# The front of a two-block transformer kernel in a new order, with other rings for its weights

## What is computed

```
def first_block(x, ...):
    n1 = rms_norm(h, norm1_gain)
    proj = n1 @ w_in                    # q_lat 512, kv_lat 256, k_pe 64, q_swa 1024, k_swa 128, v_swa 128
    q_lat, kv_lat, k_pe, q_swa, k_swa, v_swa = split(proj)
    o_mla = mla_group(...)              # 8 heads of 128+64, q and k from the latents, norm per head, rope
    o_swa = swa_group(...)              # 16 query heads of 64, 2 kv heads, window 128, bias by distance, sinks
    mixed = concat([rms_norm(o_mla, g), rms_norm(o_swa, g)])
    h = h + mixed @ w_out
    h = h + peer(rms_norm(h, norm2_gain), ...)   # product keys, top 16 of 128 x 128, 16384 experts
    return h
```

## Time and profile before

| | us |
|---|---|
| median of 3 runs | 3338.53 (3335.76 to 3339.82) |
| the profiled execution | 3337.88 |
| its span, first to last instruction | 3335.7 |
| PE busy | 3250.5 (97%) |
| VectorE busy | 2020.4 (61%) |
| ScalarE busy | 1490.8 (45%) |
| POOL busy | 539.9 (16%) |

### The profile page before, as it was taken

One profiled execution on the slowest core, in us unless ns is written; L12 is line 12 of the kernel. 1 busy time (PEld: TensorE's weight loads), 2 busy tenths in 40 slices (PEclk: granted clock), 3 DMA queues, 4 the chain that ended last, 5 costly groups with the idle time before them and its releaser, 6 DMA issues.

```text
span 3335.7 us, 38691 instructions
## 1 busy us (share of the span) xinstructions
PE 3250.5 (97%) x15278; PEld 2704.2 (81%) x15278; DVE 2020.4 (61%) x2922; ACT 1490.8 (45%) x1876; POOL 539.9 (16%) x321
## 2 busy tenths in 40 slices
PE   8888999999999999999999999999999999999998
PEld 7677898788888888888888888888888788888886
DVE  6755568884444456666666665565465655555556
ACT  5434444444444444444444444445444544444443
POOL 0100004787778700000000000000000000000000
PEclk9889999999999999999999999999999999999999
DMA  6553456888888877777776665555666566666664
GB/s 207 179 206 95 145 174 189 200 206 207 209 213 205 208 275 247 244 246 245 241 243 217 183 198 183 158 176 172 189 189 199 176 188 189 189 189 189 189 189 151
DMA packets 215092, 658.71 MB, mean 197 GB/s; under 512 B 56128, under 2 KB 56272, under 8 KB 212352
## 3 DMA queue, kind: packets, MB, share of 16 engines
q1 hardware_dynamic: 165680, 598.71, 57.6%
q0 software_dynamic: 49232, 57.54, 7.7%
HBM read 620.38 MB, written 35.78 MB: 197 GB/s over the span
## 4 chain that ended last, share of the span: by engine, by line
PE 88%; DVE 8%; ACT 3%; issue 1%; DMA 0%; DVEq 0%; ACTq 0%; SPq 0%
PE bank L1554 86%; PE bank L1616 2%; DVE wlo L1981 2%; ACT whi L1760 1%; ACT M L1802 1%; DVE AL L2027 0%; DVE M L2267 0%; DVE M L2273 0%; DVE R L2459 0%; ACT M L1750 0%; DVE M L2271 0%; DVE M L2269 0%; DVE M L2084 0%; DVE TMP L2050 0%; DVE M L2284 0%
## 5 line engine op out<-in xcount | busy, mean ns | idle before, releaser
L1981 DVE TENSOR_TENSOR wlo<-raw,whi 128x1024 fp32r<-128x1024 f32 x1101 | 1343.8, 1223 | 1082.1 <-ACT whi L1760 1077.7
L1760 ACT ACTIVATE whi<-raw 128x1024 fp32r<-128x1024 f32 x1101 | 1159.8, 1058 | 1301.5 <-PE bank L1554 1265.0
L1554 PE MATMUL bank<-whi,BH 128*128 128x512 f32 x2344 | 932.5, 398 | 12.8 <-DVE wlo L1981 7.7
L1554 PE MATMUL bank<-whi,BL 128*128 128x512 f32 x2344 | 915.3, 390 | 0.0
L1554 PE MATMUL bank<-wlo,BH 128*128 128x512 f32 x2344 | 913.8, 390 | 0.0
L1554 PE MATMUL bank<-whi,AH 128*128 128x512 f32 (+1 forms) x1952 | 772.4, 396 | 22.5 <-DVE AL L2027 15.2
L1554 PE MATMUL bank<-whi,AL 128*128 128x512 f32 (+1 forms) x1952 | 762.6, 391 | 0.0
L1554 PE MATMUL bank<-wlo,AH 128*128 128x512 f32 (+1 forms) x1952 | 762.0, 390 | 0.0
L2524 POOL DMA_INDIRECT scr_g<-M x256 | 495.0, 1934 | 437.3 <-issue 396.5
L1554 PEld LDWEIGHTS bank<-whi,BH 128*128 128x128 f32 x2344 | 440.9, 188 | 106.2 <-DVE wlo L1981 12.4
L1554 PEld LDWEIGHTS bank<-whi,BL 128*128 128x128 f32 x2344 | 440.5, 188 | 94.3
(11 more groups left out here) (240 smaller groups left out, 1600.6 us busy)
## 6 DMA issues: line engine op xcount, KB each, us to landing
raw<-in_peer_u SPq DMA_DIRECT2D x256, 512.0 KB
raw<-in_peer_v SPq DMA_DIRECT2D x256, 512.0 KB
raw<-in_w_in SPq DMA_DIRECT2D x160, 512.0 KB
raw<-in_w_up SPq DMA_DIRECT2D x128, 512.0 KB
raw<-in_w_down SPq DMA_DIRECT2D x128, 512.0 KB
raw<-in_w_out SPq DMA_DIRECT2D x64, 512.0 KB
raw<-in_w_in_a SPq DMA_DIRECT2D x32, 512.0 KB
scr_g<-M POOLq DMA_DIRECT2D x8, 2048.0 KB, 29.8
```

The source lines that it names most:

```text
L1554: return e.matmul(outp, l, r, start=start, stop=stop)
L1760: e.activation(whi[:, n % NH, :], raw[:, n % NR, :], ACT.Copy).then_inc(s_hi, 1)
L1981: e.tensor_tensor(wlo[:, n % NH, :], raw[:, n % NR, :], bf(whi[:, n % NH, :]), ALU.subtract).then_inc(s_lo, 1)
```

## The change

The eight pieces of `swa_queries(1)` move from behind w_q_b to behind w_kv_b 0, 1, and w_kv_b 2, 3 (the values) to behind w_q_b 4, 5. `bias_gen` may run from the last w_q_b gemm on. `head_norm`'s work on VectorE is three calls with yields between them, and `q_side` has one yield less behind it. `q_scale` is a task. The MLA stage no longer waits for `rows` and `halves`; its extra buffers come by a task. OM is turned in the MLA stage, as its units' outputs are done, and OS beside the first half of w_out. hold=4 is dropped in w_out. The rings have 3 raw buffers, 4 high and 4 low parts instead of 5, 3 and 3.

```diff
-    NR, NH, NST = 5, 3, 1080
+    NR, NH, NST = 3, 4, 1080
...
-        plan("w_kv_b", 0, 4)
+        plan("w_kv_b", 0, 2)
+        plan("w_in_a", 24, 8)
         plan("w_q_b", 4, 2)
+        plan("w_kv_b", 2, 2)
         plan("w_q_b", 0, 4)
-        plan("w_in_a", 24, 8)
...
-                go("head_scale", tmp, x, U, L, mul, stat(2 * U), stat(2 * U), fresh("DVE", ta))
-                tv = up("DVE", "head_scaled")
+                ss, r = stat(2 * U), stat(2 * U)
+                go("head_sum", tmp, U, ss, fresh("DVE", ta))
+                tv = up("DVE", "head_summed")
                 halves.give(TMP[:, 0:512], tv)
                 halves.give(TMP[:, 512:1024], tv)
-                box.append(tv)
+                yield
+                go("head_root", ss, U, L, mul, r, fresh("DVE", tv))
+                tv = up("DVE", "head_root")
+                yield
+                go("head_scale", x, U, L, r, fresh("DVE", tv))
+                box.append(up("DVE", "head_scaled"))
...
-                go("load_piece", n_load[0])
-                n_load[0] += 1
+                if j < NR:
+                    go("load_piece", n_load[0])
+                    n_load[0] += 1
...
+                def above(n):
+                    pair, qb, kb, c = chunks[n]
+                    go("above", n % 2, qb, kb, c, fresh("DVE", t_pos, tk[n - 2] if n >= 2 else x_read))
+                    t2[n] = up("DVE", "above")
+
+                above(0)
+                yield
+                above(1)
+                yield
...
+                    go("bias_mm", bank, n % 2, BD[:, 0:64], fresh("PE", t2[n], t_steps, bfree))
+                    tk[n] = up("PE", "bias_looked_up")
+                    yield
+                    go("bias_mask", bank, pair, c, fresh("DVE", tk[n], pair_free[pair]))
                     bias_done.append(up("DVE", "bias_masked"))
                     misc.give(bank, bias_done[-1])
+                    if n + 2 < 12:
+                        above(n + 2)
...
             def q_scale():
+                while len(t_ssq) < 6:
+                    yield
+                yield
...
-            for j in range(4):
+
+            def keys(j):
                 pair, b, last = gemm("w_kv_b", j, 2, BH[:, 4:6, :], BL[:, 4:6, :], nKV)
-                if j < 2:
-                    ts, free = take(krows)
-                    te = evac2(pair, b, last, lambda t: ts[:, t, :], free, t_kv, r=r_kv)
-                    tasks.append(k_nope(ts, te, j))
-                else:
-                    t_v += evac2(pair, b, last, lambda t: VM[:, t, 512 * (j - 2):512 * (j - 2) + 512], x_read, t_kv, r=r_kv)
+                ts, free = take(krows)
+                te = evac2(pair, b, last, lambda t: ts[:, t, :], free, t_kv, r=r_kv)
+                tasks.append(k_nope(ts, te, j))
                 step()
-            kv_free = [last]
-            tasks.append(k_rope())
-
-            for j in (2, 0, 1):
+
+            def values(j):
+                pair, b, last = gemm("w_kv_b", 2 + j, 2, BH[:, 4:6, :], BL[:, 4:6, :], nKV)
+                t_v.extend(evac2(pair, b, last, lambda t: VM[:, t, 512 * j:512 * j + 512], x_read, t_kv, r=r_kv))
+                step()
+                return last
+
+            def queries(j):
                 pair, b, last = gemm("w_q_b", 2 * j, 4, BH, BL, nQ)
                 ts, free = take(qrows)
                 te = evac2(pair, b, last, lambda t: ts[:, t, :], free, t_lat, r=r_lat)
                 tasks.append(q_nope(ts, te, j) if j < 2 else q_rope(ts, te, j))
                 step()
 
+            kv_free = []
+            keys(0)
+            keys(1)
+            a_free.append(swa_queries(1))
+            tasks.append(k_rope())
+            queries(2)
+            values(0)
+            kv_free.append(values(1))
+            queries(0)
...
+            idle.append(bias_gen())
+            queries(1)
+            tasks.append(q_scale())
             tasks.append(pairs_freed())
-            idle.append(bias_gen())
-            a_free.append(swa_queries(1))
             lend_banks()
             go("gate_blank")
             t_blank = up("POOL", "gate_blank")
             for c in range(8):
                 go("gate_clear", c, fresh("POOL", t_blank))
                 t_clear = landing("gate_cleared")
-            while len(t_ssq) < 6:
+            while len(qt_done) < 6 or len(kt_done) < 8 or not t_rq:
                 step()
-            q_scale()
-            while len(qt_done) < 6 or len(kt_done) < 8 or len(rows.free) < 2 or len(halves.free) < 2:
...
+            def more_rows():
+                while len(rows.free) < 2:
+                    yield
+                r_over = [f for _, f in rows.free]
+                for i in range(4):
+                    pml.give(Rf[:, 2048 + 512 * i:2560 + 512 * i], r_over)
+
+            tasks.append(more_rows())
+            om_done, mla_scored = {}, []
...
+            def turned_heads(x, marks, n_marks, g0, k, done):
+
+                while len(mla_scored) < 6:
+                    yield
+                for k0 in range(0, 8, 2):
+                    while len(marks(k0)) < n_marks:
+                        yield
+                    yield from trans_split(lambda kt, t: x[:, t, 128 * (k0 + kt):128 * (k0 + kt) + 128], 2, hl(AH, k + k0),
+                                           hl(AL, k + k0), lambda kt: GC[:, g0 + k0 + kt:g0 + k0 + kt + 1], marks(k0),
+                                           mla_scored, done)
+
+            nM, nS = [], []
             tasks.append(pipelined([mla_unit(0, 0), mla_unit(0, 4)] + [mla_unit(1, h) for h in range(0, 8, 2)], 6, 6))
+            tasks.append(turned_heads(OM, lambda k0: [om_done[u] for u in ((0, 4 * (k0 // 4)), (1, k0)) if u in om_done],
+                                      2, 22, 0, nM))
             finish_idle()
-            assert len(bias_done) == 12
+            assert len(bias_done) == 12 and len(nM) == 4
...
-            tasks.append(turned_heads(OM, lambda k0: [om_done[0, 4 * (k0 // 4)], om_done[1, k0]], 22, 0, nM))
+            tasks.append(turned_heads(OS, lambda k0: [os_done[u] for u in ((0, 4 * (k0 // 2)), (1, 2 * k0), (1, 2 * k0 + 2))
+                                                      if u in os_done], 3, 30, 8, nS))
...
-                pair, b, last = gemm("w_out", 4 * j, 8, AH, AL, nM, hold=4, mid=True)
+                pair, b, last = gemm("w_out", 4 * j, 8, AH, AL, nM, mid=True)
...
-            tasks.append(turned_heads(OS, lambda k0: [os_done[0, 4 * (k0 // 2)], os_done[1, 2 * k0], os_done[1, 2 * k0 + 2]],
-                                      30, 8, nS))
...
-                pair, b, last = gemm("w_out", 16 + 4 * j, 8, AH[:, 8:16, :], AL[:, 8:16, :], nS, hold=4)
+                pair, b, last = gemm("w_out", 16 + 4 * j, 8, AH[:, 8:16, :], AL[:, 8:16, :], nS)
...
-            def head_scale(tmp, x, U, L, mul, ss, r, ready):
-                for mark in ready:
-                    e.wait_ge(*mark)
-                then(e.tensor_reduce(ss.rearrange("p (t u) -> p t u", t=2), tmp, AX.X, ALU.add))
-                e.wait_ge(s_vec, at[0])
-                then(root(ss, 2 * U, L, r, mul))
-                e.wait_ge(s_vec, at[0])
+            def head_sum(tmp, U, ss, ready):
+                for mark in ready:
+                    e.wait_ge(*mark)
+                e.tensor_reduce(ss.rearrange("p (t u) -> p t u", t=2), tmp, AX.X, ALU.add).then_inc(sem("head_summed"), 1)
+
+            def head_root(ss, U, L, mul, r, ready):
+                for mark in ready:
+                    e.wait_ge(*mark)
+                root(ss, 2 * U, L, r, mul).then_inc(sem("head_root"), 1)
+
+            def head_scale(x, U, L, r, ready):
+                for mark in ready:
+                    e.wait_ge(*mark)
                 r4 = r.rearrange("p (t u) -> p t u", t=2).unsqueeze(3).to_broadcast([128, 2, U, L])
```

More of the change, by code:

```diff
@@ L593, in bias_gen @@
                 t2, tk = {}, {}
[L594 to L602, removed]
+                def above(n):
[6 more added lines that the diff above has]
+                yield
+                for n, (pair, qb, kb, c) in enumerate(chunks):
                     while pair_free[pair] is None:
@@ L605, in bias_gen @@
                     bank, bfree = yield from wait_for(misc)
-                    go("bias_mm", bank, (n - 1) % 2, BD[:, 0:64], fresh("PE", t2[n - 1], t_steps, bfree))
-                    tk[n - 1] = up("PE", "bias_looked_up")
+                    go("bias_mm", bank, n % 2, BD[:, 0:64], fresh("PE", t2[n], t_steps, bfree))
+                    tk[n] = up("PE", "bias_looked_up")
                     yield
-                    go("bias_mask", bank, pair, c, fresh("DVE", tk[n - 1], pair_free[pair]))
+                    go("bias_mask", bank, pair, c, fresh("DVE", tk[n], pair_free[pair]))
                     bias_done.append(up("DVE", "bias_masked"))
                     misc.give(bank, bias_done[-1])
+                    if n + 2 < 12:
+                        above(n + 2)
             idle.append(x_squares())
```

(29 more changed lines are left out.)

## The result

The changed kernel takes 3342.43 us (median of 20 runs, 3340.06 to 3350.39) against 3336.7 us of the kernel before in the same sessions: a ratio of 1.0019 [1.0012, 1.0026]. It is slower, by 5.7 us. I had forecast 3299; 43 us are missing.

The account below looks back on a forecast made before the run. TensorE, busy 3250.5 of 3335.7 us, was the bound, so only its idle or lower-clock time could be gained. Terms -17 - 6 - 15 + 5 - 6 = -39 against 3337.88 gave 3299 us, range 3281 to 3318.

Parts of the forecast that it names:

- Part 1: Second half of w_out: OS turned beside the first half, so the gemms no longer wait for turned rows; -17 us (15 to 18).
- Part 5: Rings, 5+3 to 3+4: low-part waits between 400 and 800 us go, -6 (-3 to -7); main loop holds, 0 (to +4).
- The load that I dated: Worst load in a gate fetch, issued at 1252.44, released ScalarE 10.7 us later; taken to leave PE 0.9 us.
- rival (d): Gate fetches: three raw buffers too few, 3 us lost at each of 16 fetches, 48 in all; 3347 us, chance 0.04.
- Part 4: Front: clears of scr_g move from 145 to about 42.5 us and share DMA with weight loads; +5 us (0 to +15).
- rival (b): Front: the clears starve the weight loads, PE loses about 15 us instead of 5; 3309 us, chance 0.16.
- Part 3: Stage A, last long projection to first MLA scores: VectorE's idle time goes, 99.9 becomes 85 us; -15 (-23 to -8).
- part 2: MLA and first half of w_out: early turning removes AL waits and most half-clock spells; -6 us (-2 to -9).
- The two waits I aimed at: PE's stage A waits: 5.09 us behind head_scale at 108.86, 6.96 for the last swa query's chain; reordering should remove both.
- rival (c): Stage A: a new wait replaces the removed one, so it gives 3 us instead of 15; 3311 us, chance 0.12.
- Rival (a): Front: loads and clears share DMA evenly, so moving the clears costs nothing; 3294 us, chance 0.15.
- rival (e): w_out: turning of OS still ends behind the first half, taking back 10 us; 3309 us, chance 0.03.

## Why the prediction was wrong

**Part 1, second half of w_out (-17): right**, by mechanism and size (-17.7). No AL wait stands in it any more.

**Part 5, the parts of the ring (-6): right, and too small.** Of the twelve wlo waits of the routing one of 0.5 us is left: PE is busy 499.55 of 500 us against 494.20, and after gains 7.9 us between 400 and 800. The runs give 9.7, with the fetches spread.

**Part 5, the main loop (0): wrong, and it decides the sign.** The failed sentence is "From issue to use a piece had ... now 6 (13.9)". It takes the ring of parts as full whenever a fetch begins. Here is the first of the 14 later fetches of after, by engine (start, us, instruction, idle before):

```profile
1209.66 0.55 POOL L2577 DMA_DIRECT2D M<-scr_a  x1 [51.86 <-DVE AL L2411]
1210.19 0.91 POOL L2578 DMA_DIRECT2D M<-scr_g  x1
...
1210.88 0.33 SPq L2617 DMA_DIRECT2D raw<-in_peer_v  x1
1211.53 0.92 SPq L2623 DMA_DIRECT2D scr_a<-M  x1
...
1208.01 0.63 ACT L1788 ACTIVATE AH<-M 128x512 fp32r<-128x512 f32 x1 [1.48 <-DVE M L2404]
1208.55 1.99 ACT L1798 ACTIVATE whi<-raw 128x1024 fp32r<-128x1024 f32 x2
1210.98 1.06 ACT L1798 ACTIVATE whi<-raw 128x1024 fp32r<-128x1024 f32 x1 [0.45 <-DMA raw<-in_peer_v]
1219.21 1.06 ACT L1798 ACTIVATE whi<-raw 128x1024 fp32r<-128x1024 f32 x1 [7.16 <-DMA raw<-in_peer_v]
...
1210.91 0.50 PE L1592 MATMUL bank<-whi,BH 128*128 128x512 f32 x1 [0.55 <-DVE wlo L2019]
1221.67 0.63 PE L1592 MATMUL bank<-whi,AH 128*128 128x512 f32 x1 [2.31 <-DVE wlo L2019]
```

ScalarE's steps for the gate wait for VectorE (1.48 here; in both kernels these waits sum to some 136 us), the splits behind them come late, and then three splits run almost in a row. At 1210.9 PE has just waited for a part: nothing is spare. The three made then last 3 x 2.76 = 8.3 us, to 1219.2. The load issued at 1210.88 releases ScalarE at 1219.21, its low part is done 2.3 us later, and PE starts at 1221.67 after 2.31 us. So it had 8.5 us from issue to use, not 13.9, and an ordinary load beside a fetch was enough; I had wanted one of over 11.6. With five raw buffers, at the same place, two pieces more had landed when the burst began. PE's one wait there is the 0.44 at the handing over, and ScalarE's next split waits for PE, not for a load:

```profile
1208.26 0.50 PE L1592 MATMUL bank<-whi,BH 128*128 128x512 f32 x1 [0.44 <-DVE wlo L2019]
```

```profile
1211.39 1.06 ACT L1798 ACTIVATE whi<-raw 128x1024 fp32r<-128x1024 f32 x1 [2.41 <-PE bank L1592]
```

It is so at nearly every fetch: 12 of the 14 are followed, 10 to 13 us after their issue, by one wait of PE for a low part (0.3 to 2.7 us). Counted piece by piece (12 matmuls each) in the traces, the first load issued beside a fetch had 8.3 to 10.8 us until its use in after, 11.0 with four raw buffers and 13.8 with five. It needs its own time, 8.6 us beside a fetch in after (median; 11.7 the longest), and 2.3 for the split. So five buffers are just enough, four nearly, and three are not.

The trace of before had this to show. The load that I dated (issued at 1252.44) and the one ahead of it, beside the same fetch, were used at 1267.23 and 1264.51 (SP, then PE):

```profile
1250.71 0.33 SPq L2573 DMA_DIRECT2D raw<-in_peer_v  x1
...
1264.51 0.39 PE L1554 MATMUL bank<-whi,AH 128*128 128x512 f32 x1
...
1267.23 0.39 PE L1554 MATMUL bank<-whi,AH 128*128 128x512 f32 x1
```

These are 14.8 and 13.8 us where my count of pieces said 16.6 for both: the ring was short by up to a piece already. Less one piece for the new ring, 12.0 and 11.0 are left, against the 10.7 + 2.3 = 13.0 that the dated load needed. Its margin was -1 us and not 0.9.

The waits of ScalarE show the turn as a whole (us in total, times, longest). Before, from 1178 to 1830 us, they were for PE, and only 9.8 us for loads of peer_v:

```profile
ACT whi L1760 <- PE bank L1554: 215.1, 138, 2.4
```

After, in the same stretch:

```profile
ACT whi L1798 <- DMA raw<-in_peer_v: 213.3, 123, 8.5
...
ACT whi L1798 <- PE bank L1592: 18.5, 9, 6.7
```

With five raw buffers the split waits for a free part; with three it waits for a load, 123 times. I had said that 9.8 us would grow to some 50 between 900 and 2200 us; it became 213 in this stretch alone. The 15 waits of PE, 18.7 us, then cost the clock too: the stretch stands at 0.98 where before stood at 1.00, which is up to 0.02 x 635 = 12.7 us of lost full speed. I had priced rival (d) at 48 us for 16 fetches and given it 0.04. It was the right mechanism at half its price, and that price was enough. That its 3347 lies near the measured 3342.43 is luck: it kept the 21 us of parts 2 and 3, of which 6.4 came.

**Part 4, the clears (+5): right mechanism, too small.** They start where I said:

```profile
41.68 0.31 POOL L2557 MEMSET M<- 128x256 f32 x1
42.29 2.29 POOL L2563 DMA_DIRECT2D scr_g<-M  x2 [0.30 <-POOL M L2557]
```

They cost 10.9 us against a place beside MLA. Against their old place I add the 3.3 us of the old order with five raw buffers, 14.2 in all, near rival (b); no run has that pair. I priced a piece at 3.7 us and gave the ring 6 us of cover. From 52 to 95 us the DMA queues of after moved (packets, MB, share; then KB and median us to landing):

```profile
q0 software_dynamic: 2740, 10.90, 69.5%
q1 hardware_dynamic: 1540, 5.65, 32.3%
...
raw<-in_w_in_a SPq DMA_DIRECT2D x9, 512.0 KB, 8.2
```

5.65 MB in 43 us are 4.0 us a piece of 0.524 MB. With five raw buffers it is 3.6:

```profile
q1 hardware_dynamic: 1726, 6.30, 36.3%
```

Without clears (new order, old rings, late clears) PE's own demand set the pace at 7.27 MB, 3.1 us a piece:

```profile
q1 hardware_dynamic: 1996, 7.27, 56.5%
```

So three loads at a time got less beside the clears than five did. The difference, 0.65 MB, is 1.2 pieces or some 4 us of PE's time, and 10.9 against 6.2 us is 4.7: most of what the clears cost more with three raw buffers. Equal turns, as I read the Trainium skill (DMA: Bandwidth & Descriptors, Queues, rings and completion order), did not come about: 1.9 to 1 in bytes. But with at most three loads out, queue 1 may have been empty at its turn, so the row does not contradict the page.

**Part 3, stage A (-15), and part 2, MLA and the first half (-6): wrong.** The two together gave 6.4. In the kernel with late clears and old rings, where nothing else disturbs, stage A runs from 92.0 to 187.7:

```profile
92.00:187.70 95.70, 73.94 (x353) 62.16 (x351) 76.21 (x151) 43.67 (x69) 0.96 (x1) 0.87 0.35 106
```

95.7 us against 99.9, at a clock of 0.87 against 0.88, and one bias chunk (1.9 us) of these 4.2 has only moved behind the first scores, as I had counted. I had said 85, as 64 to the last projection and 21 behind it. Its last projection ends at 160.5: 68.5, and then 27.2. PE's waits in this stretch:

```profile
PE bank L1592 <- DVE AL L2065: 6.0, 1, 6.0
PE bank L1654 <- DVE M L2099: 4.7, 1, 4.7
PE bank L1592 <- DVE wlo L2019: 4.4, 2, 3.4
PE bank L1592 <- DVE R L2107: 3.5, 1, 3.5
PE bank L1654 <- DVE M L2270: 3.0, 1, 3.0
```

The two waits I aimed at, 5.09 and 6.96, are gone, and others stand in their place. From 40 to 320 us PE's waits over 0.7 us sum to 36.1, before to 36.4. The failed step is that VectorE, once its waits for splits were removed, would be the bound with hardly a pause. Of the 18.5 us that it waited for high parts, 12.4 remain:

```profile
L2019 DVE TENSOR_TENSOR wlo<-raw,whi 128x1024 fp32r<-128x1024 f32 x18 | 21.9, 1223 | 12.4 <-ACT whi L1798 12.4
```

The turn below, in order of time, is no matter of the order of the pieces but of two in-order engines that wait for each other. Nor did the fourth pair of parts relieve the front, as I had held against rival (c): 20.9 us ahead behind it with four pairs, 20.6 with three.

```profile
139.50 0.63 ACT L1788 ACTIVATE TMP<-M 128x512 f32<-128x512 f32 x1 [3.16 <-DVE M L2099]
140.04 1.04 ACT L1798 ACTIVATE whi<-raw 128x1024 fp32r<-128x1024 f32 x1
...
141.11 1.23 DVE L2019 TENSOR_TENSOR wlo<-raw,whi 128x1024 fp32r<-128x1024 f32 x1 [1.73 <-ACT whi L1798]
...
142.26 0.74 DVE L2107 TENSOR_SCALAR R<-bank,ST 128x512 f32<-128x512 f32 x1
...
143.10 0.77 PE L1592 MATMUL bank<-whi,BH 128*128 128x512 f32 x1 [3.51 <-DVE R L2107]
```

A square on ScalarE waits 3.16 us for a rope on VectorE, the high part behind the square is late, the low part waits for it, the evacuation behind the low part is late, and PE waits 3.51 us for its banks. The norm in one run or in three made no difference to the time, so VectorE's pauses between the steps of the norm were no cost either. The first wait of the list above is the new tail: the first scores at 187.7 waited 6.0 us for turned rows. That is rival (c) in kind, a new wait for the removed one, and at nearly its price (it said 3 of 15; stage A gave 4, with the moved chunk). My sum for that tail had a slip, too: four of 0.68 and four of 0.47 are 4.6 us, not 3.8. In MLA the early turning did take the 4.5 us AL wait away (1.0 is left at 231.6), but a little later, at 247, in the first half of w_out, this stands instead (PE's waits, 187.8 to 346 us):

```profile
PE bank L1654 <- ACT M L1840: 6.5, 1, 6.5
```

At this place before waits 1.9 us, and after, whose clears are over by then, 3.8: so of the 4.6 us more some 1.9 come with the order and 2.7 with the clears beside it. Why the clears cost 3.3 us more there than at 145 us in the old order, where the longest wait of this kind is 2.3, stays open.

**The others.** Rival (a) falls with part 4, rival (e) with part 1. Of the checks that I listed, the wlo waits of 400 to 800 us, the first clear near 43 us and w_out without an AL wait over 1 us came out as written (of the wlo waits one of 0.5 us was left); PE did not stay over 99% busy to 2200 us (97% from 1195 to 1830). The forecast missed by 43 us: 25.3 of fetches, 14.6 of stage A and MLA (6.4 for 21), 9.2 of clears against their old place (14.2 for 5), less 3.7 in part 5 and 0.7 in part 1 are 44.7 (-39 forecast, +5.7 measured); the level of before was 1.2 lower than the 3337.88 that the sum was made against (3336.7), which leaves the 43. The range shut out the case that happened because I gave a margin of 0.9 us, worked out from one load and a full ring, a chance of 4 in 100.

## What to carry to other kernels

A ring's margin is not its depth times the pace: read it at the moment when the disturbance begins, for the engines that fill it may just have let it run dry, and a margin of under a piece deserves a large chance, not a small one. Of two rings in series, buffers that hold what has landed cover a slow transfer and buffers behind the split cover a slow split; trading one for the other pays only once the transfers are made even (a burst of 2 MB cut into eight parts paced by TensorE gave 25 us back). And when waits are removed on an in-order engine, follow the engine that waits for it in return, or the wait only changes its name.

## What was not expected of the hardware

Beside software-queued DMAs a load of 0.5 MB took 8.2 us (median, 52 to 95 us) or 9.9 (in the fetch shown above), against 4.2 between fetches (after, 1195 to 1830 us). Beside the clears the loads got more with four outstanding than with three, and no more with five: 5.65 MB in 43 us with three, 6.42 with four, 6.30 with five.

```profile
q1 hardware_dynamic: 1759, 6.42, 37.0%
```
